# Attention values of eight heads in one run of matmuls, their sums in alternating halves of one bank

## The reference

```
p = masked_softmax(einsum('bqhd,bqkd->bqhk', q_c, k_sel) * scale, mask)
o = einsum('bqhk,bqkd->bqhd', p, v_sel)
```

## Time and profile before

| | us |
|---|---|
| median of three executions | 1610.5 |
| the profiled execution, its own time | 1615.06 |
| span of the profiled execution | 1612.2 |
| TensorE busy | 1569.8 |
| VectorE busy | 1156.3 |
| ScalarE busy | 648.8 |
| GpSimd busy | 637.6 |

### The profile page before, as it was taken

The page is one execution under the profiler, slowest core; times in us unless marked ns, Lnnn a source line. Parts: engine busy times, 40 slices in busy tenths (PEclk is TensorE's granted clock), DMA queues, the critical chain, the costliest instruction groups (busy, mean ns, idle before and its releaser), DMA issues.

```text
span 1612.2 us, 24585 instructions
## 1 busy us (share of the span) xinstructions
PE 1569.8 (97%) x9008; PEld 1326.6 (82%) x9008; DVE 1156.3 (72%) x2021; ACT 648.8 (40%) x1269; POOL 637.6 (40%) x442
## 2 busy tenths in 40 slices
PE   6999999999899999999999999999999999999997
PEld 5898888888799888999887877888888888877885
DVE  5746889999556677786664276777777666678978
ACT  5544312111566577676321244222222232343445
POOL 4234654121340244433321226444544445345454
PEclk9999999999999999999999999999999999999999
DMA  6033545331515010011255422333333334574433
GB/s 229 16 93 77 120 119 161 105 104 47 155 50 131 28 54 15 15 41 41 92 154 154 131 98 66 98 99 98 98 99 109 114 97 157 199 241 153 159 104 124
DMA packets 173303, 171.10 MB, mean 106 GB/s; under 512 B 25856, under 2 KB 126208, under 8 KB 173184
## 3 DMA queue, kind: packets, MB, share of 16 engines
q1 hardware_dynamic: 172896, 169.01, 34.6%
q10 hardware_dynamic: 288, 0.52, 0.1%
HBM read 122.04 MB, written 47.45 MB: 105 GB/s over the span
## 4 chain that ended last, share of the span: by engine, by line
PE 87%; DMA 6%; DVE 3%; issue 2%; POOL 1%; ACT 1%; SPq 0%; DVEq 0%; POOLq 0%; ACTq 0%
PE psA L1663 13%; PE psA L1665 13%; PE psA L1664 13%; PE psT L1663 9%; PE psT L1664 9%; PE psT L1665 9%; PE psT L1670 7%; PE psT L1884 5%; DMA wd<-in_w_down_dram 4%; PE psA L1773 3%; PE psA L1774 3%; PE psT L1899 1%; DMA w_raw<-in_w_in_dram 1%; DMA q<-scratch_q_dsa 1%; POOL w_lo L447 0%
## 5 line engine op out<-in xcount | busy, mean ns | idle before, releaser
L447 POOL TENSOR_TENSOR w_lo<-w_raw,w_hi 128x1024 fp32r<-128x1024 f32 (+2 forms) x52 | 120.3, 2314 | 253.6 <-ACT w_hi L442 243.8
L1260 POOL TENSOR_TENSOR w_lo<-w_sum,w_hi 128x1024 fp32r<-128x1024 f32 x44 | 115.4, 2627 | 119.5 <-ACT w_hi L1545 119.5
L1482 ACT ACTIVATE s<-s,nmax 128x640 f32<-128x640 f32 (+7 forms) x192 | 144.0, 752 | 28.4 <-DVE nmax L2361 27.1
L1283 POOL TENSOR_TENSOR w_lo<-act_raw,w_hi 128x512 fp32r<-128x512 f32 x77 | 107.8, 1401 | 108.2 <-ACT w_hi L1573 108.0
L1670 PE MATMUL psT<-ident,s 128*128 128x128 f32 x816 | 120.2, 277 | 0.8 <-ACT s L1482 0.8
L442 ACT CAST w_hi<-w_raw 128x1024 fp32r<-128x1024 f32 (+2 forms) x52 | 52.7, 1017 | 145.2 <-PE psA L1665 87.4
L2582 DVE TENSOR_TENSOR w_lo<-wd,w_hi 128x512 fp32r<-128x512 f32 x77 | 92.6, 1205 | 23.7 <-ACT w_hi L1580 23.3
L2451 DVE COPY pT<-psT 128x512 f32<-128x512 f32 (+1 forms) x116 | 69.6, 600 | 54.2 <-PE psT L1670 54.1
L1670 PEld LDWEIGHTS psT<-ident,s 128*128 128x128 f32 x816 | 94.3, 141 | 16.6 <-issue 7.4
L1573 ACT CAST w_hi<-act_raw 128x512 fp32r<-128x512 f32 x77 | 47.9, 622 | 127.1 <-PE psA L1665 59.2
L2251 DVE TENSOR_SCALAR_CACHE_REDUCE equal<-score,bit_try 128x512 f32<-128x512 f32 (+2 forms) x93 | 93.7, 1008 | 0.0
(11 more groups left out here) (380 smaller groups left out, 4673.5 us busy)
## 6 DMA issues: line engine op xcount, KB each, us to landing
act_raw<-scratch_act SPq DMA_DIRECT2D x77, 256.0 KB, 3.0
w_raw<-in_w_in_dram SPq DMA_DIRECT2D x24, 512.0 KB, 4.1
scratch_act<-act SPq DMA_DIRECT2D x33, 256.0 KB, 2.1
scratch_act<-act_sum SPq DMA_DIRECT2D x33, 256.0 KB, 2.1
wd<-in_w_down_dram SPq DMA_DIRECT2D x33, 256.0 KB, 3.1
scratch_gates<-gate_out SPq DMA_DIRECT2D x32, 256.0 KB, 3.0
gates<-scratch_gates SPq DMA_DIRECT2D x30, 256.0 KB, 4.2
a<-in_w_gate_dram SPq DMA_DIRECT2D x22, 256.0 KB, 3.2
```

What stands on the lines that cost most here:

```text
L447: nc.gpsimd.tensor_tensor(lo, raw, hi.bitcast(F32), ALU.subtract).then_inc(self.lo_done, 1)
L1260: nc.gpsimd.tensor_tensor(lo2[n % RING][:], block_of(n)[:], hi2[n % RING][:].bitcast(F32), ALU.subtract)\
L1283: nc.gpsimd.tensor_tensor(lo2[slot][:, 0:512], act_raw[n % 6][:], hi2[slot][:, 0:512].bitcast(F32), ALU.subtract)\
L1482: a_.activation(s_sb[v % SR][:, 0:n], s_sb[v % SR][:, 0:n], ACT.Exp, scale=-1.0, bias=nmax[:, BR[a], i, h:h + 1], accum_out=psum_p[:, BR[a ...
```

## The change

In tiles of at most four key blocks all jobs of the eight heads are due in the step of the last group, five steps after the tile's last unit; the values of heads 0 to 3 so move four steps later. There are twelve such tiles, i = 0 to 3 of each branch. ScalarE's two copies of such a tile both stand one step after that. The groups alternate between the two halves of bank 3, and TensorE begins group o when group o - 2 is copied. Larger tiles keep their steps.

```
+    def whole_run(a, i):
+        return keys_of(a, i)[1] <= 4
-    def group_of(u, lag):
+    def groups_of(u, lag):
         a, i, h = at(u - lag)
-        return (a, i, h // G) if a and h % G == G - 1 else None
+        if not a or h % G < G - 1:
+            return []
+        if whole_run(a, i):
+            return [(a, i, g) for g in range(KV)] if h == H - 1 else []
+        return [(a, i, h // G)]
...
-            later = 0 if h % G == G - 1 else 2
+            later = H - 1 - h if whole_run(a, i) else 0 if h % G == G - 1 else 2
             values_at[u + T_LAG + 1 + V_LAG + later].append(len(jobs))
...
-        if group_of(u, O_LAG):
-            opened.append(group_of(u, O_LAG))
+        opened += groups_of(u, O_LAG)
...
-            if group_of(u, O_LAG):
-                key = group_of(u, O_LAG)
+            for key in groups_of(u, O_LAG):
...
-                a_.copy(acc[t % 2][:, 2 * P * g:2 * P * (g + 1)], psT[:, 3, 0:2 * P]).then_inc(acc_out, 1)
+                a_.copy(acc[t % 2][:, 2 * P * g:2 * P * (g + 1)], psT[:, 3, 2 * P * (o % 2):2 * P * (o % 2 + 1)]).then_inc(acc_out, 1)
...
-            if first and o >= 1:
-                pe.wait_ge(acc_out, o)
-            return psT[:, 3, 0:2 * P]
+            if first and o >= 2:
+                pe.wait_ge(acc_out, o - 1)
+            return psT[:, 3, 2 * P * (o % 2):2 * P * (o % 2 + 1)]
```

## The result

The changed kernel takes 1614.97 us (median of six executions, 1613.76 to 1618.37) against 1610.42 for the kernel before beside it: ratio 1.0024, 95% interval [1.0014, 1.0034], so 3.9 us slower by the ratio, 4.55 by the medians. The stated range ended at 1613.7; the prediction was wrong. The profiled execution is the slowest of the six: 1618.37 us, span 1616.3. In the listing of the changed kernel, scores now stand at L1779 and L1780, values at L1890, transposes at L1676, `cs` at L1929.

The account below looks back on a forecast made before the run. A query transfer until 440.3 us, then TensorE, with VectorE and GpSimd joining in win and slc tiles 0 to 3, bound the kernel; gains and losses summed to +0.81 us, forecasting 1611.3 us, range 1608.3 to 1613.7.

Parts of the forecast that it names:

- another such stretch: Waits foreseen in step 9 of win 2 may bring half clock: 4.8 us holding 2.4 us of full-speed work, 1615.7 in all.
- the second rival: Slower: moved matmuls land behind gates in slc 0-2, win 2-3; win 0-1 gains fail; +2.75, 1613.3, or 1615.7 with clock; chance 0.17.
- win 0: Run removed before cs in step 8 feeds VectorE earlier; added matmuls vanish in the wait at r: gain 0.63 us.
- win 1: As in win 0, VectorE's idle time before cs shrinks and the wait at r covers added matmuls: gain 0.87 us.
- win 2: Second cs waits for ScalarE's copy anyway; the removed run's matmuls come back in step 12: loss 1.02 us.
- slc 2: Only 0.98 of 1.61 us removed before cp is usable; 1.31 come in front of co: loss 0.33 us.
- win 3: Only 0.74 of 2.05 us removed before the second cs is used; step 12 takes 1.75 more: loss 0.68 us.
- slc 3: Effects of steps 16 and 20 on TensorE end in a 1.39 us wait for VectorE: 0.
- slc 0: Low clock makes step 16's run dearer; its removal pays about the 0.44 that step 20 costs before co: 0.
- slc 1: Removal from step 16 brings nothing, cp waits for GpSimd; 16 matmuls now stand before co in step 20: loss 0.88 us.
- dsa: Tiles 2 and 3, where TensorE never waits, each save one run's entry and exit: 0.6 us gained, bounds 0 and 0.6.
- The start: Savings in dsa 0 and 1 vanish in the wait for the queries; scores of dsa 3 begin as before: worth 0.

Follow-up runs that it names:

- more runs: Kernel before, with each pair of heads' values in a run of their own in the twelve tiles of five and more blocks; 1616.75 us, ratio 1.0031.
- the fill: Idle transposes of the identity put into TensorE's waits; changed kernel so filled 1612.28 us, kernel before so filled 1610.82 us.
- the filled one: Changed kernel with idle transposes in both its new waits and those the kernel before has too; 1612.28 us, ratio 0.9999 against the kernel before.
- `slc` alone: Against the kernel before: bank halves alternate and only the four slc tiles are merged; 1613.49 us, ratio 1.0011.
- `win` alone: Against the kernel before: bank halves alternate and only the four win tiles are merged; 1611.55 us, ratio 1.0002.
- the transposes first: Changed kernel with idle transposes, due transposes put ahead of the values in steps of merged win or slc runs; 1611.49 us, 0.9999 against the kernel before.
- the old waits filled: Changed kernel with idle transposes only in waits the kernel before has too (r of dsa 0, win 0; cp of slc 0); 1612.90 us, ratio 1.0010.
- `dsa` alone: Against the kernel before: bank halves alternate and only the four dsa tiles are merged; 1612.55 us, ratio 1.0003.

## Why the prediction was wrong

**The clock, the step that failed.** The sum was made as if TensorE's clock were the same in both kernels, and "another such stretch" stood only in the second rival, with 0.17 for all of it, on the reason that "the waits of 1.23 us at 577.77 did not bring a stretch of their own here". That was one execution. In the trace with more runs, whose tiles win 0 to 3 are those of the kernel before, the same wait did bring one, from 578.57 on; four transposes take 1.11 us there and not 0.66:

```profile
578.62 1.11 PE L1670 MATMUL psT<-ident,row_factors_wide 128*128 128x128 f32 x4 [1.24 <-POOL row_factors_wide L1232]
```

In the nine traces of unfilled kernels the clock falls in eight somewhere between 550 and 600 us, in or behind a wait, at a place or for a length that changes from one execution to the next; in the six filled in the old places it never does. The change took one such wait away, made three new ones, one of which I had foreseen, and put the long runs right behind them. The Trainium skill (TensorE: Matmul & The Clock Gate, HAM oscillation) warns of idle gaps between bursts; these traces agree in kind, but their gaps, of 1.1 to 1.8 us, are shorter than those it names. By medians on one chip the fill takes 1616.19 - 1612.28 = 3.91 us from the changed kernel and 1612.03 - 1610.82 = 1.21 from the one before: about 2.7 us of the loss are the clock, with several us of spread in the executions behind this figure. The traces bear it out: from slc 0 to win 4, half clock adds 3.5 and 3.3 us to the two of the changed kernel (against the filled one), 1.4 and 0.5 to the two of the kernel before, 2.5 more on the mean. The rest of the loss, filled against filled, is 1612.28 - 1610.82 = 1.46; it is the order of the work, forecast at 0.81.

The range did not allow for this. The bounds that I gave for the terms add up to -2.1 and +3.8 us, 1608.4 to 1614.3 and not 1609.3 to 1612.8 as I wrote; the measured 1614.97 lies above even these.

**Terms that held**, at full clock: win 0 -0.69 for -0.63, win 1 -0.72 for -0.87, win 2 +0.95 for +1.02, slc 2 +0.39 for +0.33, win 3 +0.53 for +0.68, slc 3 0 (from win 4 to slc 4, 0.03 at most). The way of working, by what ends last at each gate, was right for these. The wait of 1.79 us at the second `cs` came where it was foretold. From win 4 to the last scores the traces with merged tiles keep their shift to 0.05 us.

**slc 0**, forecast 0, was +0.41 to +0.46: about the upper bound that I gave, 0.44. I had set the 0.44 in front of `co` against a run in step 16 made dearer by a low clock; the filled traces have no such clock, and `cp` waits for GpSimd there as in slc 1 (0.24 us behind the idle transposes), so that nothing comes back.

**slc 1**, forecast +0.88, was +1.40. The step "`cp` waits for GpSimd, whose work hangs on `r` of step 13 and not on the run" holds for the run taken out of step 16. It forgot the run put into step 12: with `slc` alone the term is +0.86, with `win` alone +0.55, and the sum of the two is that of the whole. The double run holds the transposes behind it, these ScalarE's copy, and this ScalarE's exponential of the compressed scores, from which `cp` hangs; with the transposes first, 0.45 of the 0.5 are gone. The wait for GpSimd at `cp` of slc 1, foretold as over 1 us, was 0.66 (585.39 in the changed kernel): TensorE had already waited 0.79 and 0.41 us for ScalarE's exponentials just before.

**dsa**, forecast -0.60, was -0.46 to -0.54 in the four merged traces without a wait there, and -0.10 to -0.12 in the four with a wait for ScalarE's exponential, as after:

```profile
444.41 0.66 PE L1676 MATMUL psT<-ident,s 128*128 128x128 f32 x4 [0.18 <-ACT s L1488]
```

The scores behind that wait start 0.39 us later than with the old waits filled, counted from the first scores of `dsa` 3, which is all that is missing. That the light steps are too quick for ScalarE was the lower bound that I had named; why four traces have the wait and four do not was not tested.

**The start.** That `dsa` 0 and 1 are worth 0 rested on the transfer of the queries. The stretch up to `dsa` 3 took 0.61 to 2.71 us more in the eight traces with `dsa` merged (mean 1.39), 0 to 1.42 in the eight without (mean 0.53, the kernel with more runs, +0.39, among them). The two overlap, the causes seen differ (a late transfer of constants after, late queries with `dsa` alone), and the timed kernels do not tell it. It stays open whether the 0.9 us between the means belong to the change.

Summed for the traces at full clock, the terms of win and slc make +2.2 to +2.4 against +1.41 forecast. The second rival had the clock and nearly the time, 1615.7, but not its own condition: the gains of win 0 and 1 did come. That it lay near the measured time was in that part luck.

## What to carry to other kernels

A run taken out of one step and put into another must be followed twice: to what waits for the step it leaves, and to every instruction that now stands behind it, through the copy and the exponential that its neighbours feed. Where a change makes TensorE arrive early and wait, price the clock too, at the cost of the longest work behind the wait, and do not take its absence in one trace for a rule: it changes from execution to execution, and needs several traces or medians. A few idle transposes in waits that could not be removed were worth about 1.2 us here without any merging, the best part of the merging 0.9.

## What the runs showed of the hardware

Between 550 and 600 us the clock fell to 1.2 GHz in or behind waits of TensorE of 1.1 to 1.8 us, in eight of nine traces of kernels without idle transposes, and not always at the same wait. A stretch of 3.4 us at that clock cost 1.6 us where merged runs lay in it and 0.46 where TensorE would have waited 0.84 for GpSimd. Eight or twelve idle transposes (1.0 to 1.5 us) in the waits at `r` of win 0 and 1 or at `cp` of slc 0 kept the clock up in six of six traces. Entering and leaving a run of 64-column values between 128-column work cost 0.26 to 0.30 us.
